# A one-layer hybrid decoder step: how the last token tile reaches the first expert, and the order of the last output projection tile

## The reference, cut to what matters

```python
x = x + mixed @ w_o                        # output projection and residual
h = rmsnorm(x, norm_ffn)                   # what the experts read
group = argmax(h @ w_router_coarse)        # top 1 of 4 groups
e1, e2 = top2(h @ w_router_fine[group])    # top 2 of the 8 experts in it
for e in (e1, e2):                         # 32 experts in all
    gate, up = split(h @ w_expert_up[e])   # 1024 -> 2 x 256
    x += weight[e] * (silu(gate) * up) @ w_expert_down[e]   # 256 -> 1024
y = rmsnorm(x, norm_final)
```

## Time and profile before

| | |
|---|---|
| median of 3 runs | 1630.8 us (1625.7 to 1632.5) |
| the profiled execution | 1628.5 us, its span 1626.8 us |
| TensorE busy | 1521.6 us, 94% of the span |
| VectorE, ScalarE, GpSimd busy | 741.9, 376.1, 203.2 us |
| mean granted TensorE clock | 0.973 |
| moved by DMA | 273 MB |

### The profile page before, as it was taken

How to read it: one execution, slowest core, us unless ns; L and a number is a source line. 1 busy time by engine, 2 the same in 40 slices (tenths; PEclk the granted TensorE clock), 3 DMA queues, 4 the chain that set the end, 5 groups by cost and what they waited for, 6 DMA issues and landing times.

```text
span 1626.8 us, 16492 instructions
## 1 busy us (share of the span) xinstructions
PE 1521.6 (94%) x6211; PEld 964.9 (59%) x6211; DVE 741.9 (46%) x1337; ACT 376.1 (23%) x625; POOL 203.2 (12%) x224
## 2 busy tenths in 40 slices
PE   7999999989988999999999999999859999999976
PEld 6666666645665666556998766755434444444432
DVE  4667676113342534787777453264523211112116
ACT  3211101013555554321313210011111111111113
POOL 0000010000000000245278100011010000000004
PEclk9998999999999999999999999999969999999998
DMA  5264793522430112425221425433279999999938
GB/s 167 81 104 112 222 288 75 140 79 68 120 92 27 41 28 93 114 66 147 63 72 30 153 77 178 137 115 141 91 267 320 368 371 367 374 363 371 366 123 311
DMA packets 232263, 273.27 MB, mean 168 GB/s; under 512 B 62516, under 2 KB 167336, under 8 KB 231920
## 3 DMA queue, kind: packets, MB, share of 16 engines
q1 hardware_dynamic: 204628, 203.54, 40.6%
q10 hardware_dynamic: 18140, 34.48, 5.6%
q0 software_dynamic: 9408, 34.08, 5.4%
HBM read 188.83 MB, written 83.24 MB: 167 GB/s over the span
## 4 chain that ended last, share of the span: by engine, by line
PE 80%; DVE 7%; issue 4%; ACT 4%; POOL 2%; DMA 2%; POOLq 0%; ACTq 0%; SPq 0%; DVEq 0%
PE P L705 26%; PE P L1197 12%; PE P L1061 7%; PE P L1181 6%; PE P L1132 6%; PE P L862 2%; PE P L886 2%; PE P L1168 2%; POOL arena L613 1%; DVE arena L1503 1%; PE P L1105 1%; PE P L731 1%; PE P L837 1%; PE P L1085 1%; DVE arena L1505 1%
## 5 line engine op out<-in xcount | busy, mean ns | idle before, releaser
L705 PE MATMUL P<-arena 128*128 128x352 f32 (+1 forms) x1728 | 534.4, 465 | 3.9 <-ACT arena L2267 2.8
L705 PEld LDWEIGHTS P<-arena 128*128 128x128 f32 (+1 forms) x1728 | 323.6, 191 | 188.1 <-issue 29.4
L1197 PE MATMUL P<-arena 128*128 128x512 f32 x512 | 227.5, 598 | 0.8 <-ACT arena L2384 0.8
L1197 PEld LDWEIGHTS P<-arena 128*128 128x128 f32 x512 | 95.9, 192 | 109.6 <-issue 109.6
L1867 DVE COPY arena<-P 128x512 f32<-128x512 f32 x32 | 22.1, 692 | 216.2 <-PE P L1168 216.2
L1181 PE MATMUL P<-arena 128*128 128x512 f32 x256 | 115.3, 593 | 0.9 <-DVE arena L1907 0.9
L1061 PE MATMUL P<-arena 128*128 128x352 f32 x384 | 115.1, 460 | 0.7 <-DMA arena<-y_d 0.7
L1132 PE MATMUL P<-arena 128*128 128x512 f32 x224 | 101.4, 599 | 0.0
L1061 PEld LDWEIGHTS P<-arena 128*128 128x128 f32 x384 | 73.0, 190 | 41.0 <-issue 0.8
L613 POOL TENSOR_TENSOR arena<-arena,N 64x256 f32<-64x256 f32 x96 | 81.1, 845 | 48.2 <-ACT arena L2291 26.9
L1181 PEld LDWEIGHTS P<-arena 128*128 128x128 f32 x256 | 46.3, 191 | 47.4 <-issue 46.3
(11 more groups left out here) (407 smaller groups left out, 1925.0 us busy)
## 6 DMA issues: line engine op xcount, KB each, us to landing
arena<-in_w_expert_up_dram SPq DMA_DIRECT2D x32, 2048.0 KB, 12.8
arena<-in_w_expert_down_dram SPq DMA_DIRECT2D x32, 1024.0 KB, 7.7
arena<-in_w_in_dram SPq DMA_DIRECT2D x36, 512.0 KB, 4.2
x_d<-zero SPq DMA_DIRECT2D x4, 4096.0 KB, 19.7
arena<-x_d POOLq DMA_DIRECT2D x32, 512.0 KB, 5.7
y_d<-arena ACTq DMA_DIRECT2D x32, 512.0 KB, 8.0
gate_d<-arena ACTq DMA_DIRECT2D x16, 528.0 KB, 5.1
arena<-gate_d SPq DMA_DIRECT2D x24, 352.0 KB, 3.1
```

The source lines that it names most:

```text
L705: m = pe.matmul(P[0:p, b + j, 0:TBK], w[:, k, 0:p], hT[:, k, TBK * j:TBK * j + TBK], start=f, stop=l)
L1197: m = pe.matmul(P[:, i % 2, :], xgT[i % 2][:, k, :], WU[i % NWE][:, k, :], start=k == 0, stop=k == KD - 1)
```

## The change

- Tile 8's part of the output projection is written by row blocks of `W_O`: block 0 for both halves of the columns, then block 1, and so on. After block 3 a semaphore (`s_half`, which reuses `s_db`) tells SyncE that row blocks 0 to 3 are no longer needed, and SyncE asks for expert 1's up weights there. The steps of the tiles before stand at other places between the products.
- VectorE works out tile 7's slots between tile 8's residual addition and its norm, not behind it.
- Before tile 8's scatter, and once the scatters of tiles 0 to 7 have landed, GpSimd loads expert 0's rows of `x_d` to a space of their own, `xg_first` (in the down buffer 2). The scatter of tile 8 waits for that load.
- VectorE makes a 128×128 matrix `in_first` of zeros and ones: token t of tile 8 has a one at column c if it is in slot c of expert 0. (`columns`, the column numbers, is made once, long before.)
- TensorE turns the loaded rows by a product with the identity in banks 2 and 3 and adds tile 8's rows by a product of `h2` with `in_first` in the same banks. `gathered` is used from expert 1 on.
- In each up projection the wait for ScalarE's half of the transposed rows stands before the fifth product (k = 4) and not before the first.
- Expert 2's down weights wait for the copies of `xg_first`; the final norm's weights are loaded behind expert 31's.

```diff
+        xg_first = at(WR + NWE * 2048 - 2048, D)
+        first_banks = (2, 3)
...
@@ gpsimd: scatter @@
+                if p == TT_ - 1:
+                    pool.wait_ge(s_xg[0], 16)
                 for j in range(2):
                     pool.indirect_dma_start(x_d, ..., h2[p % 2][0:n, :], ...).then_inc(s_h2d[p % 2], 16)
+                if p == TT_ - 2:
+                    for b in range(2):
+                        pool.wait_ge(s_h2d[b], 32 * ((TT_ - b) // 2))
+                    pool.dma_start(xg_first, x_d[0:128, :]).then_inc(s_xg[0], 16)
...
@@ tensor: output projection @@
+                if p == TT_ - 1:
+                    for step in range(2 * KD):
+                        k, o = step // 2, step % 2
+                        m = pe.matmul(P[:, b + o, :], MIX[:, k, 128 * i:128 * i + 128], W_O[:, k, 512 * o:512 * o + 512],
+                                      start=k == 0, stop=k == KD - 1)
+                        if step == KD - 1:
+                            m.then_inc(s_half, 1)
+                        if step == 2 * KD - 1:
+                            m.then_inc(s_wt, 1)
+                        if step == 3:
+                            places(p - 2)
+                        if step == 5:
+                            h2_transposed(p - 1)
+                        if step == 8:
+                            router(p - 1)
+                    continue
...
+            def first_gathered():
+                last = TT_ - 1
+                n = rows(WORD[last])
+                pe.wait_ge(s_xg[0], 16)
+                pe.wait_ge(s_x1, TT_ - 1)
+                banks = [P[:, b, :] for b in first_banks]
+                for bank, k0 in zip(banks, (0, 4)):
+                    for k in range(4):
+                        pe.matmul(bank[:, k * 128:k * 128 + 128], xg_first[:, (k0 + k) * 128:(k0 + k + 1) * 128], ident,
+                                  start=k == 0, stop=False)
+                pe.wait_ge(s_in, IN_SET)
+                bank6()
+                bank7()
+                for bank, s_b, k0 in zip(banks, (s_6, s_7), (0, 4)):
+                    for k in range(4):
+                        m = pe.matmul(bank[:, k * 128:k * 128 + 128],
+                                      h2[last % 2][0:n, (k0 + k) * 128:(k0 + k + 1) * 128], in_first[0:n, :],
+                                      start=False, stop=k == 3)
+                    m.then_inc(s_b, 1)
...
                     pe.wait_ge(s_xgT6, i + 1)
-                    pe.wait_ge(s_xgT7, i + 1)
...
                     for k in range(KD):
+                        if k == 4:
+                            pe.wait_ge(s_xgT7, i + 1)
...
@@ vector @@
+            link(dve.tensor_tensor_scan(columns, ones[:], ones[:], -1.0, ALU.mult, ALU.add))
...
+                if p == TT_ - 1:
+                    dve.tensor_scalar(in_first, columns, slot[:, i, 0:1], Mt[:, i, 0:1], ALU.is_equal, ALU.mult).then_inc(s_in, 1)
...
                 added(p)
+                if p == TT_ - 1:
+                    places(TT_ - 2)
                 normalised(p)
-            places(TT_ - 2)
...
@@ sync @@
+            sp.wait_ge(s_half, HALF)
+            expert_up(1, 1)
             t = WORD[TT_ - 1]
             sp.wait_ge(s_h2, TT_)
...
-            sp.wait_ge(s_wt, TT_)
-            expert_up(1, 1)
             for b in range(2):
                 sp.wait_ge(s_xg[b], 16)
+            sp.wait_ge(s_wt, TT_)
             expert_up(2, 2)
+            sp.wait_ge(s_xgT6, 1)
+            sp.wait_ge(s_xgT7, 1)
             expert_down(2, 2)
```

More of the change, by code:

```diff
@@ L305, in hybrid_step @@
         PX = sb("PX", [128, 4, 2, C])
+        columns, in_first = [PX[:, i].rearrange("p a b -> p (a b)") for i in range(2)]
         N1 = sb("N1", [128, 4, HP, NC_])
@@ L360, in hybrid_step @@
         s_conv = sem("s_conv")
+        s_in, IN_SET = s_ctz, 2
         s_sq = sem("s_sq")
@@ L451, in hybrid_step @@
         s_db = sem("s_db")
+        s_half, HALF = s_db, 2 * HP + 1
         s_dr = sem("s_dr")
@@ L654, in run @@
                         pool.wait_ge(s_xgT6, i - 1)
-                    if i < E:
+                    if 0 < i < E:
                         pool.dma_start(xg[i % 2], x_d[128 * i:128 * i + 128, :]).then_inc(s_xg[i % 2], 16)
-                    else:
+                    elif i >= E:
                         pool.indirect_dma_start(xg[i % 2], None, h2_d, bass.IndirectOffsetOnAxis(idx_i[:, i:i + 1], 0)
@@ L1188, in run @@
                     pe.transpose(bank6()[:, 0:NTILE], idx_n[:], ident[0:NTILE, 0:NTILE]).then_inc(s_6, 1)
-                gathered(lo)
+                if lo == 0:
+                    first_gathered()
+                else:
+                    gathered(lo)
                 for i in range(lo, hi):
@@ L1231, in _, with bank6 @@
             n6 = [0]
-            def bank6():
+            def bank6(b=6):
                 n6[0] += 1
                 dve.wait_ge(s_6, n6[0])
-                return P[:, 6, :]
+                return P[:, b, :]
             def read6(ins):
@@ L1863, in gathered @@
             def gathered(i):
-                bk = bank6()
+                bk = bank6() if i > 0 else bank6(first_banks[0])
                 if i >= 2:
@@ L1948, in _, with bank7 @@
             pending = [[], []]
-            def bank7():
+            def bank7(b=7):
                 n7[0] += 1
                 act.wait_ge(s_7, n7[0])
-                return P[:, 7, :]
+                return P[:, b, :]
             def read7(ins):
@@ L2380, in gathered @@
             def gathered(i):
-                bk = bank7()
+                bk = bank7() if i > 0 else bank7(first_banks[1])
                 if i >= 2:
@@ L2645, in _ @@
             sp.dma_start(h2_d[128 * t:128 * t + 128, :], h2[(TT_ - 1) % 2]).then_inc(s_h2s[(TT_ - 1) % 2], 16)
-            sp.dma_start(WF, norm_final.rearrange("(a d) -> a d", a=1).broadcast_to([128, D])).then_inc(s_wf, 16)
             sp.wait_ge(s_io, 1)
@@ L2670, in run @@
                     expert(i)
+                if hi == E:
+                    sp.dma_start(WF, norm_final.rearrange("(a d) -> a d", a=1).broadcast_to([128, D])).then_inc(s_wf, 16)
             expert_tiles(sp, run)
```

## The result

The four runs of the changed kernel have a median of 1613.9 us (1609.3 to 1622.2), four of the kernel before 1628.3 us (1623.5 to 1632.5). The ratio is 0.991 with a 95% interval of 0.9885 to 0.9936: faster, by 0.6 to 1.15%.

A forecast was written before the change was run, and what follows sets the result against it. TensorE alone was taken to bound the expert stage, so time had to come from the seam ahead of it. −11.7 us plus some 0.2 for late weights gave −11.5, from a median of 1630.8 to 1619 us; range 1614 to 1626.

The forecast's parts named there:

- The chain and the rigid train: TensorE alone bounds the expert stage, 11.40 us per expert, so whatever moves the first experts moves the end.
- Part 1: Last tile of the output projection: sooner addition and moved slots, −0.35 us on everything from tile 8's transposes on.
- Part 2: Before expert 0, products replace scatter, load and transposes; first up projection ends at 1203.9 in place of 1215.60.
- the middle that was taken: Clock at the seam: full speed back between 1193.3 and 1197.5, TensorE working without a pause from 1189.87; 1195.4 taken.
- Expert 1's rows as the floor: Expert 1's load, waiting for tile 8's scatter, lands at 1203.4, so the gain is at most 12.2 us.
- Part 3: Loads: sooner load of expert 1's up weights costs 0, margin 1.9 us; expert 0's rows land 4.4 us before use.
- rival A: Expert 0's rows come late, 1627 us; only tile 7's scatter late, rows 1.5 us late, 1620.5; chance 0.07.
- late weights: Expert 2's up weights land 0.7 us late with the longest load seen; some 0.2 us in the sum.
- Middle wait: Wait before the fifth product of all 32 up projections: taken as 0, bounds 0 to 0.43 us each.
- B: The middle wait breaks the train: 0.43 us each, 13.8 us lost, 1633 us; chance 0.06.
- C: The DMA stream paces the experts, so only its 1.7 us earlier start counts: 1629 us; chance 0.09.
- D: The clock stays low through the first up projection: gain 7.7 us, time 1623 us; chance 0.12.

The follow-up runs named there:

- E5: The changed kernel with only tile 7's slots on VectorE put back behind tile 8's norm; one run of 1619.8 us.
- E9: The changed kernel with products that nobody reads in two of TensorE's waits at the seam; ratio 0.9883 to the kernel before, median 1610.7 us.
- E6: The changed kernel with expert 1's up weights asked for behind tile 8's store, as before, new product order kept; one run of 1625.4 us.
- E7: The changed kernel with the wait for ScalarE's half of the rows back before each up projection's first product; one run of 1618.1 us.
- E1: The changed kernel once more, unaltered, timed beside the kernel before; ratio 0.9921, six runs from 1615.1 to 1622.8 us.
- E10: E9 with expert 1's rows also loaded ahead and tile 8's part added by a second 0/1 matrix; one run of 1617.0 us.
- E2: The kernel before, unaltered, timed against itself; ratio 0.9981, eleven runs from 1623.6 to 1633.2 us.
- E4: The changed kernel with tile 8's output projection in the old order and expert 1's up weights asked for after it; ratio 0.9923.
- E11: The kernel before with idle products in the same two waits as E9 and 13 more in the wait for expert 0's rows; ratio 0.9957.

## Why the prediction was right and where it was wrong

- The chain and the rigid train: right. The gain arises between tile 8's products and expert 1, and 11.40 us per expert is unchanged.
- Part 1 gave 0.69 us for 0.35. The step left out that tile 8's transposes waited for bank 6, which VectorE's slots of tile 7 held behind the norm (E5). The slots in their new place cost 0.07 us (3.08 us from the addition's start to the norm's, 3.01 before), inside the 0 to 0.1 said.
- Part 2: 32 records of products at 3.27 + 2.00 us, the matrix 0.35 us (0.283 taken) and hidden, the first copy hidden. Up projection at 22.25 us behind the reference point, 23.1 forecast (1197.0 − 1173.9). Part 1 is 0.3 of the difference, the clock the rest: back 4.3 us after TensorE resumed, inside the stated 3.4 to 7.6 and 1.2 us below the middle that was taken; at half speed that is 0.6 us of work.
- Expert 1's rows as the floor: right in kind. The weight load that waits for them issues at 1210.04, 28.7 us behind the reference point, forecast 29.5: the scatter came 0.4 us sooner, and the load took 3.5 us where 3.95 was taken. TensorE reached the transposes at 29.19, so the rows were never waited for. In E9, where scatter and rows come sooner too, they are waited for (0.54 us).
- Part 3: the sooner load slows tile 6's scatter (9.3 us, 9.5 priced) at a cost of nothing, as said, and it frees tile 7's. What stands behind the second was priced in rival A alone, for a late scatter at 1.5 us: without the sooner load 3.5 us of the gain go (E6). Rows 14.4 us behind the reference point (E9) in place of 12.8, since GpSimd's first half took 1.7 us and not 1.0 and the scatter 4.4 us and not 3.6. The margin was 2.6 us, not 4.4. By the Trainium skill's rule of alternating queues ("DMA: Bandwidth & Descriptors", "Queues, rings and completion order") a scatter beside a weight load is slowed; 9.2 us beside it and 4.4 without agree. The 0.2 us for late weights did not come: expert 2's up projection at 1224.14 waited for none.
- Middle wait: 0 at the 31 others, and 1.1 us gained at expert 0, 0.84 of them its copy (E7). The forecast's chain has the up projection straight behind the products, so this saving was in its sum, though it is not named there.
- Rivals. A did not occur; E6 makes its late scatter, and cost 3.5 us, between A's 7.5 and the 1.5 of its milder form: the load of the rows took 4.5 us, not 9.9. B fell by E7. C fell: the period is 11.40 us with the train 12.5 us nearer, and in E9 with it 15.7 us nearer (43.94 − 28.21), where C allowed 1.7. D fell in the changed kernel: full speed at 1201.3, the up projection at 1203.58.
- Size: the seam gave 12.5 us where 11.5 were forecast. The mis-sized terms are part 1 (0.3 us too small), the clock's return (0.6) and the late weights (0.2).

**The step that failed is the lower end of the range**: "The range: below, the floor of 12.2 us with the lower runs, 1614". Both of its terms were too small. The first, "the gain is at most 1215.60 − 1203.4 = 12.2", took expert 1's rows at 29.5 us behind the reference point; they were there at 28.7, so the most that could be gained was 13.0 us, and 12.5 were. The second, "the lower runs", left some 2.3 us (1628.5 − 12.2 = 1616.3, and down to 1614; the lowest of the three runs known lay 2.8 us below the profiled one). A kernel's runs lie 12 to 13 us apart, in step with their time at half speed, and the first four runs of the changed kernel had 75 us of it on average, the next six 82.5 (median 1618.0). Medians of four and of six such runs differ by 4 us.

That the median fell just outside, by 0.1 us, is chance. Over all ten runs the median is 1616.8 us, 2.2 us under the forecast; the ratio of E1, 0.9921, is a gain of 12.9 us of 1630. Why the clock falls here or there in one execution and not in the next stays open; no run varied it.

## What to carry to other kernels

When data makes a round trip to HBM only to be put in order, the last part can enter by a product with a 0/1 matrix while the earlier part is loaded ahead; look then at what runs beside it, since a weight load beside the scatter ahead of it cost 3.5 us here. Price a serial seam at the clock that is granted there, and try idle products in its waits: idle products in two waits took a further 3.2 us off this seam, and that kernel, at 0.9883 of the time before, is the best version of this study; in E10 the clock fell in spite of them. And before a range is given, look at how far runs of the same kernel lie apart, and measure a local distance in the trace, which repeated to 0.15 us where whole runs moved by 10.

## What the runs showed of the hardware

- A run's time follows its time at half clock by 0.33 to 0.41 us per us, over 64 and 10 runs; that time varies by 30 us between executions of one kernel (64 to 94 us, and 75 to 108 us). This is a correlation; no run set it.
- A scatter of 128 rows by GpSimd's indirect DMA landed in 3.3 to 3.6 us by itself (tile 7's in E5, tiles 6's and 8's in the kernel before), in 4.4 us where a 512 KB store was issued 1.1 us ahead of it (tile 7's in the changed kernel), and in 9.2 to 10.3 us beside a 2 MB weight load on SyncE's queue (second halves of tile 7's in the kernel before, E2, E4, E6 and E11). A plain load of 512 KB that began some 2 us before such a weight load landed took 4.5 us in E6 and 3.6 in E4, against 3.7 without one.
- The instruction of tile 7's first scatter half kept GpSimd busy for 1.68 us where it was issued during VectorE's norm of a 128×1024 tile (the changed kernel), and for 0.97 us in E5 and in the kernel before, where it came behind the norm. What in the norm does it was not tried.
- A wait inside an accumulation chain of TensorE for something long done costs nothing that a period of 11.40 us shows.
